# Delta layer of an eight-layer model: a head's preparation inside the preceding head's levels, and the recurrence's step ahead of the triangles' products

## Chip, cores and metric

One core of a Trainium2 chip runs the whole program in one launch. The metric is the device time of that launch in microseconds (us), the median of several runs.

## What is computed

Eight layers over 512 tokens of width 1024 in fp32; the seventh is the delta layer of this case. For each of 6 heads (width 128) and both directions of time it solves a gated delta rule. The reference, cut to that:

```python
g = jnp.cumsum(g, axis=-1)
decay = jnp.exp(jnp.where(tril, g[..., :, None] - g[..., None, :], NEG_INF))
k_beta = k * beta[..., None]
lmat = jnp.where(strict, jnp.einsum('bhnik,bhnjk->bhnij', k_beta, k) * decay, 0.0)
a = lmat + jnp.eye(DN_CHUNK)
sol = lax.linalg.triangular_solve(a, rhs, left_side=True, lower=True, unit_diagonal=True)
intra = jnp.where(tril, jnp.einsum('bhnik,bhnjk->bhnij', q, k) * decay, 0.0)
def step(state, inp):
    v_new = uc - jnp.einsum('bhck,bhkv->bhcv', wc, state)
    out = einsum(qc * exp(gc), state) + einsum(ac, v_new)
    state = state * exp(g_last) + einsum(kc * exp(g_last - gc), v_new)
o = o_fwd + o_bwd
o = o * lax.rsqrt(jnp.mean(o * o, axis=-1, keepdims=True) + EPS) * out_norm * jax.nn.silu(z)
```

## The kernel before

The kernel works with chunks of 128 tokens, 4 for each head (`TT = 4`, `P = 128`, `S = 512`, `NH = 6`), and with one list of instructions written out by hand for each engine (`pe`, `act`, `dve`, `pool` of `dn_layer`, L2231 to L2722). Semaphores tie them; each engine takes its own list strictly in order. PSUM has eight banks, `PS[:, 0..7, :]`.

The loop over h runs from 0 to 6. Turn h holds three things.

**Preparation of head h.** TensorE multiplies the gate column with a triangle to spread the cumulated gates (L2398, banks 2 and 3, one for each direction), forms keys by keys and keys by queries (L2405, banks 0 and 1), and turns values and keys (L2415, bank 7, one after the other). VectorE subtracts the columns and adds the causal mask (L2654), ScalarE takes the exponentials (L2499, L2501), VectorE weighs them with beta (L2660, L2664), multiplies with the key product to give NT (L2669) and with the query product to give AT (L2672). TensorE turns NT (L2424), ScalarE copies it to M (L2522). VectorE's two copies with a mask (L2677, L2679) put the neighbours of the diagonal into the unit triangles TT and Tm, which GpSimd has set to the identity (L2571, L2577). GpSimd also multiplies the queries with the gates (L2583, L2587).

**Levels 1 to 6 of head h** double the size of the inverted blocks. A level is four hops on TensorE for two halves g of the chunks: hops 0 and 1 multiply NT with Tm and M with TT into banks 0 and 1 (L2314, L2317); ScalarE copies a bank to XZ (L2528); hops 2 and 3 multiply XZ with Tm and TT into banks 2 and 3 (L2324, L2327); VectorE copies the result under a mask into Tm and TT (L2695, L2696), which the next level's hops read. Level 6 makes only TT. In level 1 a run of the mask is 2 elements, then 4, 8 and so on.

**Recurrence of head h-1**: four steps c, each for two directions, each in three hops (`recur_pe`): state products (L2346, L2348), the product of TT with the residual (L2355), the update and the output products (L2360, L2361). Between them stand VectorE's residual (L2686), ScalarE's scaling with beta (L2515) and VectorE's state (L2704, L2707), the last behind both halves' level copies. Step 0 stands in the preparation of head h, steps 1 to 3 in levels 1 to 3, a recurrence hop behind each of the level's hops 1, 2 and 3. After step 3 ScalarE squares the output in bank 6 (L2537), TensorE sums it with a matrix of ones over 128x512 (L2440), ScalarE takes the root (L2540), and VectorE at level 5 takes the reciprocal over 128x512 (L2713) and gates and splits the output (L2714 to L2718), ahead of its copies of level 6.

Turn 6 has only the recurrence of head 5. Behind it the output projection starts.

Of the kernel before, what the change touches and what calls it, by code (L numbers as in the profile page):

```python
# [14 lines left out]
F32 = mybir.dt.float32  # L15
# [3 lines left out]
ALU = mybir.AluOpType  # L19
# [3 lines left out]
P = 128  # L23
# [21 lines left out]
NH = 6  # L45
# [15 lines left out]
def program(nc, io, out):  # L61
    ctx = ExitStack()
    with ctx:
# [2167 lines left out]
        def dn_layer(l):  # L2231
            q = sig("dn", "conv gdve gact gcol mask gr prep eg D Dx nt at "
                    "vte qg ti head root ve rm")
# [22 lines left out]
                     W=([P, S],), S=([P, 2, P],), r=([P, 2, P],), vn=([P, 2, P],), sq=([P, S],)))  # L2256
            NT, M = hT_a[:, 5, :], hT_b[:, 5, :]
            Tm, XZ = hT_a[:, 6:8, :], hT_b[:, 6:8, :]
# [44 lines left out]
            def invert_pe(h, lv, hop):  # L2303
                t_ = nc.tensor
                g = hop % 2
                TTh = d_.TT[:, h % 2]
                if hop < 2:
# [3 lines left out]
                    if lv == 1 and g == 1:  # L2311
                        t_.wait_ge(q.at, 2 * h + 2)
# [17 lines left out]

            def recur_pe(h, c, hop):
                t_ = nc.tensor
                for d in range(2):
# [3 lines left out]
                    if hop == 0:  # L2337
                        if c == 0 and d == 0:
                            if h:
                                t_.wait_ge(q.os, B.os + h)  # L2340
                            t_.matmul(PS[:, 6, :], r.zr[0:1, :], r.zr[0:1, 0:1].to_broadcast([1, S]), start=True, stop=False)
# [7 lines left out]
                    elif hop == 1:  # L2349
                        if c:  # L2350
                            t_.wait_ge(q.rr, B.rr + j + 1)
                        elif d == 0:
                            t_.wait_ge(q.pc, joined(h, NL - 1, 1))
                        rhs = d_.r[:, d, :] if c else d_.v[:, h % 2, cc]
# [10 lines left out]
            def pe():  # L2365
# [23 lines left out]
                nh.pe()  # L2389
                for h in range(NH + 1):  # L2390
                    if h < NH:
                        t_.wait_ge(q.gdve, 4)
                        t_.wait_ge(q.nrm, L0 + 2 * h + 2)
                        for d in range(2):
                            if h:
                                t_.wait_ge(q.pc, joined(h - 1, NL - 1, d))
                            for c in range(TT):
                                mm = t_.matmul(PS[:, 2 + d, cs(c)], r.g[:, c, NH * d + h:NH * d + h + 1].to_broadcast([P, P]),  # L2398
                                               r.tri[:, d, :], start=True, stop=True)
                            mm.then_inc(q.gr, 1)  # L2400
                        if h == 0:
                            t_.wait_ge(q.nrm, L0 + 2 * NH)
                        for n, rhs in enumerate((HP + h, h)):
                            for c in range(TT):
                                mm = t_.matmul(PS[:, n, cs(c)], r.qkvT[:, HP + h, cs(c)], r.qkvT[:, rhs, cs(c)], start=True, stop=True)  # L2405
                            mm.then_inc(q.prep, 1)
                        if h:
                            t_.wait_ge(q.kte, B.kte + h)
                        if h >= 2:
                            t_.wait_ge(q.root, 2 * h - 2)  # L2410
                        for n in (2 * HP + h, HP + h):
                            if n < 2 * HP:
                                t_.wait_ge(q.vte, h + 1)
                            for c in range(TT):
                                mm = t_.transpose(PS[:, 7, cs(c)], r.qkvT[:, n, cs(c)], ident[:])  # L2415
                            mm.then_inc(q.prep, 1)
                    if h:
                        recur_pe(h - 1, 0, 0)
                        recur_pe(h - 1, 0, 1)
                    if h < NH:  # L2420
                        t_.wait_ge(q.nt, h + 1)
                        t_.wait_ge(q.eg, 2 * h + 1)
                        for c in range(TT):
# [404 lines left out]
```

## Time and profile before

| | us |
|---|---|
| median of 3 runs | 2932.04 (2931.57 to 2935.28) |
| the profiled execution's own time | 2930.64 |
| its span, first to last instruction | 2928.5 |
| TensorE busy in the span | 2623.7 |
| weight loads / VectorE / ScalarE / GpSimd busy | 2125.6 / 1449.2 / 1068.6 / 268.6 |
| mean granted TensorE clock | 0.935 |

The heads' loop of the delta layer runs from 2165.5 us (first decay product) to 2503.1 us (first product of the output projection). A product of 128x128 by 128x128 in fp32 stands in the trace as two records of MATMUL and two of LDWEIGHTS; a transposition stands as one. "MATMUL x8" is four products. The granted clock is a share of TensorE's 2.4 GHz: 1.00 is that level, 0.50 is 1.2 GHz, a value between them is a mean over both.

### The profile page before, as it was taken

The numbers are of one execution on the slowest core, as the hardware profiler recorded it, in microseconds if no ns is written. First come the engines' busy times: TensorE is split into PE (matmuls) and PEld (weight loads), VectorE is DVE, ScalarE is ACT, GpSimd is POOL, SyncE is SP. The second block draws the span as 40 slices with busy tenths as digits, with TensorE's granted clock in tenths as the row PEclk, the third lists the DMA queues.
The fourth block names the chain that finished last, engine by engine and source line by source line (L and its number), as shares of the span: only waits on it lengthen the run. The fifth ranks groups of instructions, "written<-read, shape, count | busy, mean of one in ns | idle before, by whom it ended". The sixth has DMA issues, their size and how long they took to land.

```text
span 2928.5 us, 33226 instructions
## 1 busy us (share of the span) xinstructions
PE 2623.7 (90%) x13178; PEld 2125.6 (73%) x13178; DVE 1449.2 (49%) x2374; ACT 1068.6 (36%) x1873; POOL 268.6 (9%) x420
## 2 busy tenths in 40 slices
PE   6898999999789989999789999999778687899998
PEld 4677777788357777877468888888547676688887
DVE  5667565653484556532335333257445555443422
ACT  3445432422463455444424222242433333332221
POOL 5233021020000132000000000010000100000000
PEclk7999999999799999999789999999779788999999
DMA  5522273364012311330103333232200000233332
GB/s 207 180 71 88 80 253 128 102 218 141 30 37 73 130 37 58 107 91 30 44 29 108 101 94 95 87 116 83 68 1 1 1 1 1 65 94 101 94 94 79
DMA packets 146227, 250.16 MB, mean 85 GB/s; under 512 B 15455, under 2 KB 65914, under 8 KB 145049
## 3 DMA queue, kind: packets, MB, share of 16 engines
q1 hardware_dynamic: 129008, 198.08, 21.8%
q0 software_dynamic: 14816, 48.31, 5.0%
q8 instruction: 105, 1.72, 0.2%
q10 hardware_dynamic: 2249, 1.65, 0.2%
q14 instruction: 49, 0.40, 0.0%
HBM read 245.84 MB, written 5.30 MB: 86 GB/s over the span
## 4 chain that ended last, share of the span: by engine, by line
PE 75%; DVE 10%; ACT 8%; DMA 4%; issue 2%; POOL 0%; SPq 0%; DVEq 0%; ACTq 0%
PE PS L218 19%; PE PS L220 18%; PE PS L219 18%; PE PS L985 2%; ACT tmp L752 1%; PE PS L2314 1%; PE PS L2317 1%; DMA hT_b<-in_w_mod 1%; PE PS L2327 1%; PE PS L2324 1%; PE PS L1760 1%; ACT w_hi L203 1%; PE PS L1445 1%; DVE x L808 1%; PE PS L1744 1%
## 5 line engine op out<-in xcount | busy, mean ns | idle before, releaser
L210 DVE TENSOR_TENSOR w_lo<-w_raw,w_hi 128x1024 fp32r<-128x1024 f32 (+1 forms) x344 | 412.5, 1206 | 779.1 <-ACT w_hi L203 777.9
L203 ACT ACTIVATE w_hi<-w_raw 128x1024 fp32r<-128x1024 f32 (+1 forms) x344 | 356.6, 1045 | 1039.3 <-DMA w_raw<-in_ffn_w_gate_up 308.0
L218 PE MATMUL PS<-hT_hi,w_hi 128*128 128x512 f32 (+1 forms) x1728 | 661.0, 383 | 21.5 <-DVE hT_lo L820 13.7
L220 PE MATMUL PS<-hT_hi,w_lo 128*128 128x512 f32 (+1 forms) x1728 | 652.7, 378 | 0.0
L219 PE MATMUL PS<-hT_lo,w_hi 128*128 128x512 f32 (+1 forms) x1728 | 652.3, 378 | 0.0
L218 PEld LDWEIGHTS PS<-hT_hi,w_hi 128*128 128x128 f32 x1728 | 331.0, 192 | 85.1 <-issue 19.3
L220 PEld LDWEIGHTS PS<-hT_hi,w_lo 128*128 128x128 f32 x1728 | 330.4, 191 | 59.4
L219 PEld LDWEIGHTS PS<-hT_lo,w_hi 128*128 128x128 f32 x1728 | 331.0, 192 | 56.8 <-issue 0.2
L218 PE MATMUL PS<-w_hi,hT_hi 128*128 128x512 f32 (+1 forms) x704 | 289.9, 412 | 35.3 <-DVE hT_lo L2722 9.1
L219 PE MATMUL PS<-w_lo,hT_hi 128*128 128x512 f32 (+1 forms) x704 | 278.4, 395 | 0.0
L220 PE MATMUL PS<-w_hi,hT_lo 128*128 128x512 f32 (+1 forms) x704 | 278.0, 395 | 0.0
L218 PEld LDWEIGHTS PS<-w_hi,hT_hi 128*128 128x128 f32 x704 | 140.9, 200 | 71.4 <-issue 15.8
L219 PEld LDWEIGHTS PS<-w_lo,hT_hi 128*128 128x128 f32 x704 | 141.1, 200 | 26.9 <-issue 1.8
L220 PEld LDWEIGHTS PS<-w_hi,hT_lo 128*128 128x128 f32 x704 | 140.1, 199 | 27.9
L517 DVE SCALAR_TENSOR_TENSOR macc<-mraw,cond,macc 128x512 f32<-128x512 f32 x160 | 122.0, 762 | 37.5 <-DMA mraw<-in_w_mod 34.7
L218 PE MATMUL PS<-w_hi,ffn_hi 128*128 128x512 f32 x352 | 139.4, 396 | 0.0
L219 PE MATMUL PS<-w_lo,ffn_hi 128*128 128x512 f32 x352 | 139.2, 396 | 0.0
L220 PE MATMUL PS<-w_hi,ffn_lo 128*128 128x512 f32 x352 | 139.2, 395 | 0.0
L462 POOL DMA_DIRECT2D mraw<-in_w_mod x160 | 86.3, 540 | 420.3 <-DVE macc L517 417.5
L985 PE MATMUL PS<-gla_E 128*128 128x128 f32 x448 | 62.6, 284 | 21.1 <-DVE gla_E L1204 21.0
L985 PEld LDWEIGHTS PS<-gla_E 128*128 128x128 f32 x448 | 58.4, 196 | 31.6 <-issue 29.3
L220 PEld LDWEIGHTS PS<-w_hi,ffn_lo 128*128 128x128 f32 x352 | 66.2, 188 | 15.9
(546 smaller groups left out, 3546.9 us busy)
## 6 DMA issues: line engine op xcount, KB each, us to landing
w_raw<-in_ffn_w_gate_up SPq DMA_DIRECT2D x176, 256.0 KB, 3.1
mraw<-in_w_mod POOLq DMA_DIRECT2D x160, 256.0 KB, 4.0
w_raw<-in_gla_w_in SPq DMA_DIRECT2D x48, 512.0 KB, 4.7
w_raw<-in_ffn_w_down SPq DMA_DIRECT2D x44, 512.0 KB, 3.8
w_raw<-in_fox_w_in SPq DMA_DIRECT2D x32, 512.0 KB, 4.3
w_raw<-in_sgu_w_in SPq DMA_DIRECT2D x24, 512.0 KB, 4.7
w_raw<-in_dn_w_in SPq DMA_DIRECT2D x24, 512.0 KB, 3.6
w_raw<-in_gla_w_out SPq DMA_DIRECT2D x16, 512.0 KB, 4.5
```

Source lines behind the costliest of these rows:

```text
L203: nc.scalar.activation(w_hi[:, n % NS, :, 0:m], w_raw[:, n % NS, :, 0:m], ACT.Copy).then_inc(w_hidone, 1)
L210: nc.vector.tensor_tensor(w_lo[:, n % NS, :, 0:m], w_raw[:, n % NS, :, 0:m], w_hi[:, n % NS, :, 0:m].bitcast(F32), ALU.subtract).then_inc( ...
L218: nc.tensor.matmul(o, l_hi, r_hi, start=start, stop=False)
L219: nc.tensor.matmul(o, l_hi, r_lo, start=False, stop=False)
L220: return nc.tensor.matmul(o, l_lo, r_hi, start=False, stop=stop)
L462: eng.dma_start(mraw[:, n % MS, 0, :], w[:, i % KT, m * BW:(m + 1) * BW]).then_inc(p_landed[n % MS], 16)
L517: nc.vector.scalar_tensor_tensor(out=acc, in0=mraw[:, n % MS, 0, :], scalar=cond[:, i % KT:i % KT + 1], in1=acc, op0=ALU.mult, op1=ALU.add ...
L752: ins = a.activation(tmp[:, k * P:(k + 1) * P], PS[:, 2 * t + k // 4, (k % 4) * P:(k % 4 + 1) * P], ACT.Identity, scale=nxt.scale[:, k:k + 1],
L808: v.tensor_tensor(x[:, t, :], x[:, t, :], y, ALU.add).then_inc(x_done, 1)
L985: mm = pe_.matmul(PS[:, l % 2, ts], a, m, start=True, stop=True)
L1445: t_.matmul(PS[0:nr, bank, :], sums[:, nr - per * n:2 * nr - per * n], sq(n), start=n == 0, stop=n == n_tiles - 1).then_inc(lens.sum, 1)
L1744: t_.matmul(PS[:, w.u % 3, 0:w.n], w.q, w.k, start=True, stop=True).then_inc(su.sc, 1)
```

## The change

The preparation of head n = h + 1 is spread over the levels of head h, on all engines. Preparation of head 0 stands before the loop. In each turn of level and hop TensorE takes the recurrence's hop first and the triangles' product after it; the recurrence has one step in each of levels 1 to 4. For this:

- NT, M and Tm exist twice (`NTs`, `Ms`, `Tms`), by the parity of the head. The decays live in M's place or in a spare tile, the second exponential has a tile of its own (`eb`).
- Banks: both directions' gates, the key product, the turned NT and the spread root all use bank 7; the query product bank 4; the turned values and keys bank 5; sums of squares four columns of bank 6.
- The neighbour copy of 128x512 is now two copies of 128x256, every second element of a row into one matrix each.
- Sums and root: four products with one column (`sums_pe`), root and reciprocal over 128x4, then four products that spread the reciprocal over a bank (`spread_pe`), one turn later. The gate is two products in place in `szT` (`gate_dve`, parts 0 and 2) with the split as part 3.

The diff of the parts that order the work; the bodies of the decay, products, weighing and key steps are those of before with the new banks and tiles:

```diff
-            NT, M = hT_a[:, 5, :], hT_b[:, 5, :]
-            Tm, XZ = hT_a[:, 6:8, :], hT_b[:, 6:8, :]
+            NTs, Ms = (d_.W[:], hT_a[:, 5, :]), (hT_b[:, 4, :], hT_b[:, 5, :])
+            Tms, XZ = (hT_a[:, 6:8, :], hf), hT_b[:, 6:8, :]
+            decay = lambda n, d: hT_a[:, 4, :] if d else Ms[n % 2]
...
+            def decay_pe(n, d):
+                t_ = nc.tensor
+                if d:
+                    t_.wait_ge(q.eg, 2 * n + 1)
+                elif n >= 3:
+                    t_.wait_ge(q.free, 2 * n - 4)
+                for c in range(TT):
+                    mm = t_.matmul(PS[:, 7, cs(c)], r.g[:, c, NH * d + n:NH * d + n + 1].to_broadcast([P, P]),
+                                   r.tri[:, d, :], start=True, stop=True)
+                mm.then_inc(q.gr, 1)
...
+            def sums_pe(k):
+                t_ = nc.tensor
+                t_.wait_ge(q.root, 3 * k + 1)
+                t_.wait_ge(q.free, 2 * k + 1)
+                for c in range(TT):
+                    mm = t_.matmul(PS[:, 6, c:c + 1], d_.sq[:, cs(c)], ones[:, 0:1], start=True, stop=True)
+                mm.then_inc(q.head, 1)
+
+            def spread_pe(k):
+                t_ = nc.tensor
+                t_.wait_ge(q.root, 3 * k + 3)
+                if k < NH - 2:
+                    t_.wait_ge(q.te, B.te + k + 3)
+                for c in range(TT):
+                    mm = t_.matmul(PS[:, 7, cs(c)], d_.rt[:, c:c + 1].to_broadcast([P, P]), ident[:], start=True, stop=True)
+                mm.then_inc(q.head, 1)
...
                 for h in range(NH + 1):
...
+                    n = h + 1
                     for lv in range(1, NL):
                         for hop in range(4):
+                            if h and lv <= TT and hop:
+                                recur_pe(h - 1, lv - 1, hop - 1)
                             if h < NH:
-                                if lv == 1 and hop == 3:
-                                    t_.wait_ge(q.eg, 2 * h + 2)
                                 invert_pe(h, lv, hop)
-                            if h and lv < TT and hop:
-                                recur_pe(h - 1, lv, hop - 1)
...
+                            if h >= 2 and lv == 1 and hop == 1:
+                                spread_pe(h - 2)
+                            if h and lv == 6 and hop == 1:
+                                sums_pe(h - 1)
+                            if n < NH:
+                                if lv == 4 and hop == 2:
+                                    products_pe(n, 0)
+                                if lv == 5 and hop == 1:
+                                    products_pe(n, 1)
+                                    rows_pe(n, 0)
+                                if lv == 6 and hop == 1:
+                                    rows_pe(n, 1)
+                        if n < NH:
+                            if lv == 1 or lv == 2:
+                                decay_pe(n, lv - 1)
+                            if lv == 5:
+                                upright_pe(n)
+                    if h == NH:
+                        spread_pe(h - 1)
...
                     for lv in range(1, NL):
...
+                        if h and lv <= TT:
+                            recur_act(h - 1, lv - 1)
+                        if n < NH:
+                            if lv == 2 or lv == 3:
+                                decay_act(n, lv - 2)
+                            if lv == 5:
+                                values_act(n)
+                            if lv == 6:
+                                upright_act(n)
+                                keys_act(n)
+                        if h and lv == 6:
+                            a.wait_ge(q.head, 3 * h - 1)
+                            a.activation(d_.rt[:], PS[:, 6, 0:TT], ACT.Sqrt, scale=1.0 / P, bias=r.eps[:]).then_inc(q.root, 1)
...
+                def neighbours_dve(n, side):
+                    mask = lvl[:, 0, :].rearrange("p (b h) -> p b h", h=2).unsqueeze(1).to_broadcast([P, TT, P // 2, 2])
...
+                    for e in range(2):
+                        rows = into[:, e, :].rearrange("p (c b h) -> p c b h", c=TT, h=2)[:, :, :, e]
+                        ins = v.copy_predicated(rows, mask[:, :, :, e], off.rearrange("p (c b h) -> p c b h", c=TT, h=2)[:, :, :, e])
...
                 for h in range(NH + 1):
...
+                    n, k = h + 1, h - 1
+                    for lv in range(1, NL):
+                        if h and 2 <= lv <= TT:
+                            residual_dve(k, lv - 1)
+                        if h >= 2 and lv <= 2:
+                            gate_dve(k - 1, lv + 1)
+                        if n < NH:
+                            if lv == 2 or lv == 3:
+                                decay_dve(n, lv - 2)
+                            if lv == 4 or lv == 5:
+                                weigh_dve(n, lv - 4)
+                            if lv == 5:
+                                keys_dve(n)
+                            if lv == 6:
+                                neighbours_dve(n, 0)
+                        if h < NH:
+                            level_dve(h, lv)
+                        if h and lv < TT:
+                            state_dve(k, lv - 1)
+                        if h and lv == 5:
+                            gate_dve(k, 0)
+                        if n < NH:
+                            if lv == 5:
+                                queries_dve(n)
+                            if lv == 6:
+                                neighbours_dve(n, 1)
+                        if h and lv == 6:
+                            gate_dve(k, 1)
```

## Rows read from the trace of the kernel before

**Rows 1.** The page's head.

```profile
span 2928.5 us, 33226 instructions
```

**Rows 2.** Turns of the loop: length, busy by engine (instructions), clock, DMA.

```profile
core 0: us, PE busy (x) PEld busy (x) DVE busy (x) ACT busy (x) POOL busy (x), PEclk, DMA share, GB/s
2186.20:2227.40 41.20, 32.91 (x233) 30.57 (x233) 22.05 (x44) 12.52 (x28) 3.85 (x4) 0.91 0.00 1
2227.40:2281.50 54.10, 40.17 (x292) 37.87 (x292) 31.35 (x62) 18.24 (x38) 5.02 (x6) 0.87 0.00 1
2281.50:2335.90 54.40, 40.52 (x292) 38.22 (x292) 31.24 (x62) 18.35 (x38) 5.02 (x6) 0.82 0.00 1
...
2390.50:2445.10 54.60, 40.74 (x291) 38.43 (x291) 31.23 (x61) 18.32 (x38) 5.02 (x6) 0.84 0.00 1
2445.10:2480.50 35.40, 30.81 (x235) 29.30 (x235) 18.62 (x39) 13.21 (x29) 0.00 (x0) 0.93 0.00 1
2480.50:2503.10 22.60, 12.69 (x71) 10.21 (x71) 12.21 (x22) 5.17 (x11) 0.00 (x0) 0.81 0.00 1
```

**Rows 3.** Chain of waits, turn 2: start, length, what ran.

```profile
2309.48 3.25 DVE dn_sq L2713
...
2316.04 3.75 PE PS L2398 x16
```

**Rows 4.** Shorter stretches, columns as in rows 2.

```profile
2196.68:2200.55 3.87, 3.87 (x34) 3.77 (x33) 1.55 (x4) 1.20 (x2) 0.00 (x0) 1.00 0.00 0
2344.11:2349.92 5.81, 5.81 (x55) 5.81 (x53) 3.14 (x10) 1.82 (x4) 0.00 (x0) 1.00 0.01 3
...
2371.00:2374.50 3.50, 3.45 (x18) 3.48 (x19) 1.36 (x5) 0.00 (x0) 0.00 (x0) 0.56 0.00 0
...
2224.50:2227.40 2.90, 0.11 (x1) 0.00 (x0) 2.90 (x3) 0.00 (x0) 0.00 (x0) 0.97 0.00 0
...
2228.00:2230.50 2.50, 2.50 (x14) 2.50 (x13) 0.00 (x0) 0.60 (x1) 0.00 (x0) 0.51 0.03 7
```

**Rows 5.** Small operations elsewhere: shortest/median/longest in ns, first and last start.

```profile
L504 PE MATMUL PS<-ones,macc x32: 352/352/352, 38.2 to 44.8; 128*128 128x1 f32 x32
...
L1160 DVE RECIPROCAL stat<-stat x8: 159/164/177, 196.9 to 1161.6; 128x4 f32<-128x4 f32 x8
```

**Rows 6.** Masked copies and the weighing, columns as in rows 5.

```profile
L2696 DVE COPY_PREDICATED dn_TT<-lvl,PS x72: 429/435/773, 2191.8 to 2480.1; 128x256 f32<-128x256 int8 x72
...
L2677 DVE COPY_PREDICATED dn_TT<-lvl,hT_a x6: 2347/2366/2370, 2181.6 to 2440.5; 128x512 f32<-128x512 int8 x6
...
L2679 DVE COPY_PREDICATED hT_a<-lvl,hT_b x6: 2555/2560/2560, 2183.6 to 2442.5; 128x512 f32<-128x512 int8 x6
...
L2660 DVE TENSOR_SCALAR dn_W<-dn_AT,dn_nbeta x24: 278/284/1290, 2175.0 to 2435.2; 128x128 f32<-128x128 f32 x24
```

**Rows 7.** Groups by line, turn 2: busy us, mean ns, idle before and its releaser.

```profile
L2398 PE MATMUL PS<-dn_tri,dn_g 128*128 128x128 f32 x16 | 3.8, 429 | 4.6 <-DVE dn_TT L2696 4.6
...
L2415 PE MATMUL PS<-ident,dn_qkvT 128*128 128x128 f32 x8 | 1.3, 279 | 0.7 <-ACT dn_v L2492 0.7
...
L2664 DVE SCALAR_TENSOR_TENSOR dn_W<-dn_AT,dn_nbeta,dn_W 128x128 f32<-128x128 f32 x4 | 2.1, 594 | 0.0
...
L2672 DVE TENSOR_TENSOR dn_AT<-dn_AT,PS 128x512 f32<-128x512 f32 x2 | 1.3, 678 | 0.0
L2714 DVE SCALAR_TENSOR_TENSOR tmp<-PS,vrows,dn_sq 128x512 f32<-128x512 f32 x1 | 0.8, 751 | 0.0
...
L2669 DVE TENSOR_TENSOR hT_a<-dn_W,PS 128x512 f32<-128x512 f32 x1 | 0.7, 686 | 0.0
...
L2499 ACT ACT_TABLE_LOAD x1 | 1.3, 1283 | 0.0
...
L2507 ACT ACTIVATE dn_ks<-PS,dn_kd 128x128 f32<-128x128 f32 x4 | 1.2, 408 | 0.0
```

**Rows 8.** Chain of waits at the start of the loop, columns as in rows 3.

```profile
2165.58 3.71 PE PS L2398 x16
...
2186.21 1.22 PE PS L2314 x4
```

More of the change, by code:

```diff
@@ new lines, in recur_act @@
+                def recur_act(k, step):
+                    for d in range(2):
+                        c = step if d == 0 else TT - 1 - step
+                        a.wait_ge(q.vm, B.vm + (TT * k + step) * 2 + d + 1)
+                        a.activation(d_.vn[:, d, :], PS[:, 4 + d, P:2 * P], ACT.Identity,
+                                     scale=r.beta[:, c, NH * d + k:NH * d + k + 1]).then_inc(q.ve, 1)
+                for d in range(2):
+                    decay_act(0, d)
+                values_act(0)
@@ new lines, in dve, with decay_dve @@
+                v.wait_ge(q.nrm, L0 + 2 * NH)
+                def decay_dve(n, d):
+                    v.wait_ge(q.gr, 2 * n + d + 1)
+                    for c in range(TT):
+                        ins = v.scalar_tensor_tensor(out=decay(n, d)[:, cs(c)], in0=PS[:, 7, cs(c)],
+                                                     scalar=r.G[:, d, c, n:n + 1], in1=r.cm[:, d, :],
+                                                     op0=ALU.subtract, op1=ALU.add)
+                    ins.then_inc(q.D, 1)
@@ new lines, in weigh_dve @@
+                def weigh_dve(n, d):
+                    W = NTs[n % 2]
+                    v.wait_ge(q.Dx, 2 * n + d + 1)
+                    for c in range(TT):
+                        if d == 0:
+                            ins = v.tensor_scalar(W[:, cs(c)], decay(n, 0)[:, cs(c)], r.nbeta[:, c, n:n + 1], None, ALU.mult)
+                        else:
+                            ins = v.scalar_tensor_tensor(out=W[:, cs(c)], in0=decay(n, 1)[:, cs(c)],
+                                                         scalar=r.nbeta[:, c, NH + n:NH + n + 1], in1=W[:, cs(c)],
+                                                         op0=ALU.mult, op1=ALU.add)
+                    then_dve(ins)
@@ new lines, in dve @@
+                for d in range(2):
+                    decay_dve(0, d)
+                for d in range(2):
+                    weigh_dve(0, d)
+                keys_dve(0)
+                queries_dve(0)
+                for side in range(2):
+                    neighbours_dve(0, side)
+                for h in range(NH + 1):
+                    n, k = h + 1, h - 1
[26 more added lines that the diff above has]
+                            gate_dve(k, 1)
@@ L2720, in dve @@
+                for part in (2, 3):
+                    gate_dve(NH - 1, part)
                 for n in range(2):
```

325 lines of the change are left out of this document (143 added, 182 removed).

## The prediction

> **What bounds the kernel now.** I read the page first: one core, a span of 2928.5 us [rows 1]. The change touches one stage, the delta layer's loop over its six heads, so I cut that stage into its turns [rows 2]. Each turn begins where head h's first level product starts. A turn with both a head's levels and the preparation of the next takes 54.1 to 54.6 us, four times (three stand in the rows); the first takes 41.2 us (no recurrence beside it), the last head's 35.4 us (nothing to prepare), and the tail, recurrence of head 5 alone, 22.6 us. In a 54.4 us turn TensorE is busy 40.5 us at a granted clock of 0.82, VectorE 31.2, ScalarE 18.4, GpSimd 5.0: no engine is full. The chain of waits says why [rows 3]. From 2281.5 to 2309.5 it runs on TensorE. Then it passes to VectorE's reciprocal over 128x512 (3.25 us) and the gate behind it; TensorE, through with level 6, waits 4.6 us for the last copy into TT queued behind them [rows 7]. From 2316.04 to 2335.88, 19.8 us, it is the preparation in series: decay products, exponentials, weights, two neighbour copies.
>
> The second thing to see is what TensorE costs inside the levels [rows 4]. A level with a recurrence step, 26 products of 128x128, took 5.81 us with TensorE busy all of it at clock 1.00: 0.2235 us a product. A level alone, 16 products, took 3.87, 0.3 more than the products. So levels are bound by TensorE already, and whatever is put among them costs its own TensorE time.
>
> **The change, part by part.** For a middle head (h = 2 to 4) TensorE now issues in one turn: 88 inversion products, 34 of the recurrence, 8 decay, 8 for the two key products, 4 for the spread row: 142 x 0.2235 = 31.7 us. Beside them 12 transposes, by the group of 8 at most 0.12 each at the full clock, 1.4; the zero product 0.25; and four one-column sums, 8 records. One column does not make a product cheap: 32 records took from 38.2 to 44.8 us at the low clock [rows 5], 0.21 each, so I estimate half at the full clock, 8 x 0.11 = 0.9. Together 34.3 us. That is the floor of a turn, by level: 6.95, 6.7, 5.8, 6.25, 5.4, 3.2.
>
> Removed from the path: the preparation as a stage (19.8 us), and the wide reciprocal. In its place stands one over 128x4, 0.164 us in the nearest row [rows 5], after a square root over 128x4.
>
> Now who comes late. I laid the four instruction queues side by side, with durations from [rows 6, 7] and 0.2 us for each handover.
> - Level 2: the recurrence's step now stands ahead of the second triangle product. Its state copy stands in VectorE's queue behind the copies of level 1: 0.4 us. The second decay product waits for ScalarE's exponential of the first (they share bank 7), behind the 1.28 us table load: 0.5.
> - Level 4: no decay product stands between level 3 and the step that needs the new state, which VectorE makes after both level copies: 0.7. Before the change two triangle products covered this. This is the cost of putting the recurrence first.
> - Levels 5 and 6: VectorE has in its queue the weights of the second direction (2.1 us), the key product (0.7), four level copies (0.44 each), the gate's first product (0.75), two query products (1.3), then neighbour copies, level 6, neighbour copies again. The last release the next turn. TensorE has 5.4 + 3.2 us of work there. VectorE reaches the gate 6.4 us after level 5 begins and the first neighbour copy 8.45 us after. TensorE loses 0.4 at level 5, 0.65 at level 6, and then waits for neighbours.
> - Next turn: the zero product waits for the square root, which stands on ScalarE behind eight scaled key copies (2.3 us) and a table load: 0.35.
>
> **The neighbour copies** are the one price I don't have. Before: 128x512 with the source in SBUF, 2.37 and 2.56 us, in runs of one element that alternate between two matrices [rows 6]. After: four copies of 128x256, stepping two elements, within one matrix. Bounds: 0.44 us, the median of a 256 copy with runs of four or more; 1.19, half of the old one. I take 0.75, what the 256 copies of level 1 (runs of two) show as the maximum in the same row. Then the neighbours of side one are done 12.35 us after level 5 began; TensorE had finished at 9.6: 2.95 us of idle time.
>
> The Trainium skill, "Vector Engine (DVE) Microarchitecture Reference", section "Measured stream behaviour on trn2", speaks against the cheap end: a port keeps its rate only for adjacent pairs of words, and small steps on sources or destination cost up to 2.5 ns a column. As an estimate from that page, 256 columns would take 0.6 to 0.7 us and the forecast fall by about 3 us. No row here has this shape.
>
> Stalls together: 0.4 + 0.5 + 0.7 + 0.4 + 0.65 + 2.95 + 0.35 = 5.95. A turn is 34.3 + 5.95 = 40.25.
>
> **The clock.** After an idle stretch of 2.9 us (2224.5 to 2227.4) the granted clock fell to 0.51 over 2228.0 to 2230.5; after the 4.6 us idle it was 0.56 over 2371.0 to 2374.5 [rows 4]. My idle of 2.95 is of that size. 3.5 us at about half rate lose 1.7 us. I include it: 42.0 us a turn.
>
> **GpSimd beside VectorE.** The weights' scaling took 0.284 us in the median and 1.290 at most [rows 6], one of each four caught while GpSimd multiplied the queries. GpSimd's multiplications move along, and in my layout meet the weights again, so I keep the 2.1 us for four [rows 7]. The Trainium skill, "SBUF — State Buffer", section "SBUF: two separate sides", has it as an exclusive lock of a shared port pair; the trace agrees in the one slow copy of four. Its reach to the neighbour copies, with two SBUF inputs, no row shows. By my layout GpSimd is idle there; a collision would cost up to 1.2 us a turn.
>
> **Other stretches.** Start: first decay product at 2165.5, first level product at 2186.2 [rows 8]. The copies shorten by 4.9 - 3.0 = 1.9, the exponentials no longer stand behind v's copy and a table load (1.9), the second half of the chain shortens by the products already waiting; against it decay 1 now waits for exponential 0. Queue by queue I get 2182.2: -4.0, bounds -1 and -6. First turn: levels 1 to 4 take 18.2 us of the present 24.8 (levels 5 and 6: 6.6), the fills add 1.6 beyond the slack, and levels 5 and 6 take 11.8 (12.55 without the gate's 0.75): 31.6 instead of 41.25: -9.65. Second turn: no spread product, no late gate: 40.8 for 54.0: -13.2. Third to fifth: 3 x 42.0 for 163.7: -37.7. Last head, nothing to prepare, level by level with the stalls and the clock: 8.1 + 6.2 + 5.8 + 6.0 + 4.1 + 3.3 = 33.5 for 35.4: -1.9. Tail: reciprocal 3.35 and first gate product off the path, but first gate product (0.95), sums (1.1) and spread (1.1) enter it: -1.8.
>
> **Sum.** 4.0 + 9.65 + 13.2 + 37.7 + 1.9 + 1.8 = 68.3. The stage moves next to nothing by DMA [rows 2], and the projection behind it starts when its last operand is split, so I shift it whole. The profiled execution's 2930.6 gives 2862.3. The median of the runs is 1.4 us higher: 2864.
>
> **Rivals.**
> 1. *TensorE's floor.* The queues fit, nothing waits, the clock holds: 34.3, 33.4 and 29.7 us for turns, 31.0 for head 5. That saves about 102 us: 2830. For it: the levels ran at full load before. Against: VectorE's 6.6 us at level 5 and the neighbours behind it. Chance 0.10.
> 2. *Cheap copies and a clock that holds*: 0.44 us copies shorten a turn by 1.2, the clock by 1.7: -16 us, 2848. Chance 0.20.
> 3. *The old rate stays*: 1.19 us a copy, six heads at 1.76: +10.6, 2874. Chance 0.15.
> 4. *It doesn't do what it says.* An engine's queue is in order; if a wait for a preparation step (bank 7 is used five times a turn, each use behind another engine's read) stands ahead of level work at every level, the preparation stays in series and only the gate's 4.6 us go: 5 x 5 = 25 us, 2907. Against it: GpSimd and ScalarE work less than half of a turn [rows 2]. Chance 0.08.
> 5. *Slower: the clock.* A turn holds 34.3 us of TensorE work at the full clock. If small stalls everywhere keep it at the low level (0.5), each microsecond of this work takes two. The turn had 14.4 us to give (54.4 - 40.0), so it turns slower once 42% of that work runs low; wholly low it would be 34.3 + 40.25 = 74.6, 5 x 20 = 100 us slower, 3030. Against: four levels in a row are full of work, and the levels of before, no fuller, ran at 1.00 [rows 4]. Chance 0.04.
>
> The forecast has 0.43: 2852 to 2874. The range of 2836 to 2888 leaves out the floor, most of rival 4 and rival 5. A measurement of this kernel can tell about 0.2% (6 us) from no change. Faster by more than that: 0.94; within it: 0.02; slower: 0.04.
>
> **What would show it.** Right: middle turns of about 42 us; a gap on TensorE before the first level product, released by VectorE's neighbour copies, of about 3 us; the clock near 0.5 for 3 us behind it; neighbour copies at 0.6 to 0.9 us; a 0.7 us wait before the recurrence's state product at level 4; no 3.3 us reciprocal. Wrong: a turn under 37 us (VectorE kept up), or above 46 (waits in bank 7 or on GpSimd, to be seen as decay or key products waiting on ScalarE).

## The result, and the profile after

The changed kernel takes 2857.48 us (2855.09 to 2861.78, 4 runs); the kernel before took 2932.12 us beside it. The ratio is 0.9745, interval 0.9728 to 0.9762. The profiled execution took 2855.09 us with a span of 2853.4 us, 75.1 less than before. The forecast was 2864, with a range of 2836 to 2888, and faster by over 0.2%. The kernel is faster by more than that, and its time lies in the range, 6.5 us under the forecast.

The turns of the loop in the changed kernel, cut as in [rows 2] (length, busy us and instructions of TensorE, its weight loads, VectorE, ScalarE and GpSimd, then clock, DMA share, GB/s):

```profile
2182.30:2212.40 30.10, 27.47 (x220) 26.78 (x220) 17.79 (x45) 11.91 (x26) 4.22 (x5) 0.94 0.00 1
2212.40:2252.60 40.20, 38.19 (x297) 36.64 (x297) 22.36 (x58) 15.34 (x36) 4.83 (x6) 0.92 0.01 1
2252.60:2292.90 40.30, 37.88 (x305) 36.44 (x305) 24.24 (x62) 17.86 (x39) 4.83 (x6) 0.96 0.01 1
2292.90:2331.70 38.80, 36.38 (x306) 34.93 (x306) 24.24 (x62) 17.88 (x39) 4.83 (x6) 1.00 0.00 1
2331.70:2373.40 41.70, 39.37 (x306) 37.71 (x306) 24.15 (x62) 17.89 (x39) 3.68 (x4) 0.92 0.01 2
2373.40:2406.50 33.10, 31.72 (x261) 30.13 (x261) 14.85 (x38) 10.90 (x24) 0.00 (x0) 1.00 0.00 1
2406.50:2428.10 21.60, 14.78 (x97) 12.45 (x95) 11.55 (x28) 4.64 (x11) 0.00 (x0) 0.85 0.00 1
```

A middle turn fell from 54.4 us to 38.8 to 41.7. TensorE is now busy nearly all of it. The three middle turns (the third, fourth and fifth of these rows) hold the same instructions and differ only in the clock: 1.00 in the shortest. Of the 15.6 us between 54.4 and 38.8, 11.5 are idle time of TensorE that is gone (13.9 before, 2.4 now). The other 4.1 are its own busy time, which fell from 40.5 to 36.4 although it issues 14 records more: the clock was 0.82 in that turn before [rows 2] and is 1.00 here.

From the first level product to the first product of the output projection the stage takes 245.8 us; before it took 316.9 (2186.2 to 2503.1). Below I compare kernels by this length first: the loop starts up to 8 us earlier or later from one execution to the next (2181.2 us in one execution of this kernel, 2182.3 in another, 2189.5 in a kernel with the same work ahead of it), which has nothing to do with the stage.

What TensorE waits for between 2182 and 2428 us (waiting line, releaser, us in total, times, longest):

```profile
PE PS L2313 <- DVE tmp L2734: 6.2, 3, 2.6
PE PS L2313 <- DVE hT_a L2734: 6.0, 3, 2.4
PE PS L2362 <- DVE dn_szT L2773: 1.6, 1, 1.6
PE PS L2396 <- DVE dn_S L2765: 1.3, 6, 0.2
PE PS L2337 <- ACT ajunk L2530: 1.1, 3, 0.4
```

L2313 is the first level product, L2734 the neighbour copies: six waits of 12.2 us. One of them, 2.4 us, ends where the stage begins; the five inside it take 2.64, 1.80, 1.80, 1.81 and 1.72 us. The rest is small. The wait for the last TT copy behind the reciprocal (4.6 in [rows 7]) is gone.

The end of a middle turn, from the timeline (start, length, what; in brackets the idle time before and its releaser):

```profile
2288.70 1.02 PE L2362 MATMUL PS<-ones,dn_sq 128*128 128x1 f32 x8
2288.74 1.16 POOL L2617 COPY hT_a<-ident 128x512 f32<-128x512 f32 x2 [2.52 <-PE PS L2313]
2289.66 1.41 DVE L2734 COPY_PREDICATED dn_TT<-lvl,hT_a 128x256 f32<-128x256 int8 x2
2290.05 1.06 PE L2326 MATMUL PS<-dn_TT,hT_b 128*128 128x128 f32 x8
2290.88 0.79 DVE L2746 COPY_PREDICATED dn_TT<-lvl,PS 128x256 f32<-128x256 int8 x2
2291.58 1.28 DVE L2734 COPY_PREDICATED tmp<-lvl,hT_b 128x256 f32<-128x256 int8 x2
2292.91 0.75 PE L2313 MATMUL PS<-tmp,hT_a 128*128 128x128 f32 x4 [1.80 <-DVE tmp L2734]
```

TensorE ends level 6 at 2291.1. VectorE still has the last level copies (L2746) and the second pair of neighbour copies in its queue, and the next head's first product waits 1.80 us.

### The profile page after: what moved, and what is told of

It reads as the page before. It is cut to its first block, busy times and chain, and to the rows that moved or that the text cites. A ratio compares the mean times of both kernels' runs of the same rounds, so it can differ in the third digit from the quotient of the medians.

```text
span 2853.4 us, 33398 instructions
## 1 busy us (share of the span) xinstructions
PE 2613.5 (92%) x13262; PEld 2121.6 (74%) x13262; DVE 1406.8 (49%) x2386; ACT 1063.3 (37%) x1871; POOL 269.0 (9%) x420
## 4 chain that ended last, share of the span: by engine, by line
PE 77%; DVE 8%; ACT 8%; DMA 4%; issue 2%; POOL 0%; SPq 0%; DVEq 0%; ACTq 0%
PE PS L218 20%; PE PS L219 19%; PE PS L220 19%; PE PS L985 2%; ACT tmp L752 1%; PE PS L2313 1%; DMA hT_b<-in_w_mod 1%; DVE x L808 1%; PE PS L1760 1%; PE PS L2326 1%; PE PS L2323 1%; PE PS L2316 1%; PE PS L1445 1%; ACT w_hi L203 1%; PE PS L1744 1%
## 5 line engine op out<-in xcount | busy, mean ns | idle before, releaser
L517 DVE SCALAR_TENSOR_TENSOR macc<-mraw,cond,macc 128x512 f32<-128x512 f32 x160 | 122.2, 764 | 39.0 <-DMA mraw<-in_w_mod 36.4
L2570 ACT ACTIVATE hT_b<-PS 128x512 f32<-128x512 f32 (+1 forms) x72 | 40.5, 562 | 113.5 <-PE PS L2316 99.0
```

Source lines behind the costliest of these rows:

```text
L517: nc.vector.scalar_tensor_tensor(out=acc, in0=mraw[:, n % MS, 0, :], scalar=cond[:, i % KT:i % KT + 1], in1=acc, op0=ALU.mult, op1=ALU.add ...
L2570: a.activation(XZ[:, g, 0:m], PS[:, g, 0:m], ACT.Copy).then_inc(q.xe, 1)
```

## The experiments

In the diffs minus is the changed kernel unless another is named. Where a kernel issues products or a reciprocal that nobody reads, its text says so; nothing else of the computation is left out anywhere.

**The same kernel again.**

> The changed kernel itself again, for the runs of the same chip. Both theories: 2855 to 2862 us. Theory A (the granted clock falls after TensorE's 1.8 us wait for the neighbour copies, in some turns and not in others) also expects turns between 38.8 and 41.7 us, with other turns the long ones than in the first profile. Rival B (the long turns are long because of their place) expects turns 1, 2 and 4 long again and 3 short.

2857.25 us (2854.61 to 2860.78), stage 245.8 us. Turns of 31.2, 38.7, 41.8, 38.8 and 40.2 us, where the first execution had 30.1, 40.2, 40.3, 38.8 and 41.7. Theory A is half right. The work is the same and the lengths differ, so the clock makes the difference; but it fell in the same turns again, the second, third and fifth, as rival B had it, and the fourth and the last head's stayed at 1.00. (38.7 is long for the second turn: it takes 37.3 without a fall, see the next run.) What changed is how long a fall lasts: about 7, 3 and 7 us in the first execution, 3, 7 and 3 in this one.

Here are stretches of 2 us in four turns of the first execution, columns as above. The second and fourth lie in turns without a fall:

```profile
2254.60:2256.60 2.00, 2.00 (x11) 2.00 (x11) 0.00 (x0) 0.31 (x1) 0.00 (x0) 0.50 0.00 0
2294.90:2296.90 2.00, 2.00 (x19) 2.00 (x19) 0.24 (x1) 0.61 (x2) 0.00 (x0) 1.00 0.00 0
2333.70:2335.70 2.00, 2.00 (x10) 2.00 (x11) 0.00 (x0) 0.02 (x1) 0.00 (x0) 0.50 0.04 8
2375.40:2377.40 2.00, 2.00 (x19) 2.00 (x19) 0.23 (x1) 0.60 (x2) 0.00 (x0) 1.00 0.00 0
```

All four begin some 2 us after the 1.7 to 1.8 us wait at a turn's start. TensorE is busy in all of them and issues 19 records of products in two stretches and 10 or 11 in the other two. So the same wait lets the clock fall from 1.00 to 0.50 in some turns and not in others. Why in these turns stays open: in the kernel with the order put back, below, it fell in the second, fourth and fifth turn, with the same waits of 1.7 to 2.6 us.

**The gap filled.**

```diff
+                            if lv == 6:
+                                for c in (0, 1, 2, 3, 0, 1, 2, 3):
+                                    t_.matmul(PS[:, 0, 256 + P * (c % 2):384 + P * (c % 2)], NTs[h % 2][:, cs(c)], ident[:], start=True, stop=True)
```

> Adds eight products without use (1.8 us at the full clock) behind the last triangle product of level 6, where TensorE waits 1.8 us for the neighbour copies. Theory A (that wait makes the granted clock fall in three of five turns, 1.5 to 2.9 us each): all turns at about 38.8 us, 4 to 8 us faster than the changed kernel although it does more work. Rival B (the clock falls for another reason, or not from this wait): no gain, or up to 2 us slower.

2851.41 us (2846.35 to 2856.89), ratio to the kernel before 0.9729 (0.9708 to 0.9749), stage 237.8 us, 8.0 less. Its turns 2 to 4:

```profile
2216.50:2253.80 37.30, 36.98 (x314) 35.73 (x314) 22.40 (x58) 15.32 (x36) 4.84 (x6) 1.00 0.01 1
2253.80:2292.50 38.70, 38.08 (x321) 36.64 (x321) 24.28 (x62) 17.79 (x39) 4.85 (x6) 1.00 0.00 1
2292.50:2331.30 38.80, 38.12 (x321) 36.68 (x321) 24.29 (x62) 17.88 (x39) 4.85 (x6) 1.00 0.01 1
```

Eight products without use most likely make the kernel faster. The turn does not get shorter than a clean one (VectorE is as late as before); only the falls are gone. Turn by turn that gives 0, 3.0, 1.5, 0, 3.0, and 0.5 in the last head and tail, together 8.0 us. The intervals of the two ratios overlap, so the gain in the whole time is likely, not certain; the absence of the falls is plain in the trace, which is one execution.

**The order put back**: triangles' product first, the recurrence's hop behind it.

```diff
-                            if h and lv <= TT and hop:
-                                recur_pe(h - 1, lv - 1, hop - 1)
                             if h < NH:
                                 invert_pe(h, lv, hop)
+                            if h and lv <= TT and hop:
+                                recur_pe(h - 1, lv - 1, hop - 1)
```

> Undoes the second half of the change: in each level and hop TensorE takes the triangles' product first, the recurrence's hop after it. Theory A (the recurrence is off the path either way; TensorE's work is the same): within 3 us of the changed kernel, the 0.2 us wait for the state at level 4 gone, nothing else. Rival B (the order is what lets the preparation fit in): the recurrence's values come 0.9 us later in each step, ScalarE and VectorE stand idle for them, and the turns grow by 1 to 3 us each: 5 to 15 us slower than the changed kernel.

2855.95 us (2848.55 to 2861.19), ratio 0.9737 (0.9714 to 0.9759), stage 243.3 us: no difference that can be told. The waits show why:

```profile
PE PS L2313 <- DVE tmp L2734: 6.2, 3, 2.6
PE PS L2313 <- DVE hT_a L2734: 6.0, 3, 2.4
PE PS L2337 <- ACT ajunk L2530: 3.8, 3, 1.3
```

The wait for the new state (L2396) is gone, as expected, but the second decay product, behind the level, now waits 1.28 us instead of 0.38 for ScalarE's exponential of the first. In a middle turn they cancel (38.9 us clean, against 38.8): level 3 begins 0.8 us later in the turn, and levels 4 and 5 together take 0.7 less. In the last head's turn, which has no decay products, putting the order back gains: the spread product of head 4 starts 31.8 us after the head's first product instead of 34.0, at clock 1.00 in both.

**The neighbour copies ahead**: of VectorE's level 6 copies and of the second query product. The core of it; a wait of the recurrence's first step is raised to cover the later query product.

```diff
                             if lv == 6:
                                 neighbours_dve(n, 0)
+                                neighbours_dve(n, 1)
...
                             if lv == 5:
-                                queries_dve(n)
+                                queries_dve(n, (0,))
                             if lv == 6:
-                                neighbours_dve(n, 1)
+                                queries_dve(n, (1,))
```

> VectorE makes the neighbour copies ahead of the copies of level 6 and of the second query product. Theory A (these copies are the last release of a turn): the wait ahead of the first level product shrinks from 1.8 to about 0.6 us, 6 us over five turns, and with it the clock's falls, up to 7 more: 6 to 13 us faster than the changed kernel. Rival B (something else is due at the same time, such as ScalarE's keys and root): under 2 us.

2855.7 us (2851.03 to 2857.03), ratio 0.974 (0.9721 to 0.9758), stage 245.3: the wait fell from 1.80 to 1.50 us only.

```profile
PE PS L2313 <- DVE dn_TT L2746: 7.9, 6, 2.1
```

The releaser has changed from the neighbour copies to the last copy into TT. Both count on the same semaphore `pc`, so a wait for the neighbours' count holds for every copy queued on it, whatever the order. That is a flaw of this experiment, and that it gained so little says nothing against the queue as the cause. So the next kernel gives the neighbour copies a semaphore of their own.

**The same with its own semaphore**, against the last kernel:

```diff
+                    if lv > 1:
+                        t_.wait_ge(q.pc, joined(h, lv - 1, g))
+                    elif g == 0:
+                        t_.wait_ge(q.nb, h + 1)
...
-                        ins.then_inc(q.pc, 1)
+                        ins.then_inc(q.nb, 1)
```

> The order of copies_first (both neighbour copies ahead of the copies of level 6 and of the second query product), but with a semaphore of their own, so that the first level product is not held by the count of the level copies. Theory A (the last release of a turn is the second neighbour copy, when nothing stands ahead of it): the wait shrinks from 1.8 to about 0.6 us, the clean turn from 38.8 to 37.6, and the clock falls in fewer turns or none: 6 to 12 us faster than the changed kernel, 2845 to 2851. Rival B (ScalarE's copy of the turned matrix, or its root, is due at the same time): the wait stays above 1.4 us and the time within 3 us of the changed kernel.

2851.42 us (2849.09 to 2857.35), ratio 0.9731 (0.9717 to 0.9746), stage 240.6. The interval overlaps the changed kernel's. The wait did not shrink to the expected 0.6 us, nor the turn to 37.6.

```profile
PE PS L2394 <- ACT dn_rt L2586: 3.7, 4, 1.3
PE PS L2316 <- DVE tmp L2737: 2.8, 3, 1.5
PE PS L2316 <- DVE hT_a L2737: 1.8, 2, 0.9
```

The wait for neighbours halved to 0.9 us in a middle turn, and the turn kept its length, 38.7 us at clock 1.00. The stage is shorter because the first turn's wait shrank (2.64 to 1.48) and because the clock fell in two turns, the second and the fifth, and not in three. The 0.9 us come back as a wait of the zero product (L2394) for ScalarE's root, which stands behind the scaled key copies and a table load. The predicted "root" term had been hidden behind the neighbours until then.

**The root ahead of the scaled keys**, against the last kernel:

```diff
                             if lv == 6:
                                 upright_act(n)
-                                keys_act(n)
                         if h and lv == 6:
                             a.wait_ge(q.head, 3 * h - 1)
                             a.activation(d_.rt[:], PS[:, 6, 0:TT], ACT.Sqrt, scale=1.0 / P, bias=r.eps[:]).then_inc(q.root, 1)
+                        if n < NH and lv == 6:
+                            keys_act(n)
```

> copies_own with ScalarE taking the square root ahead of the eight scaled key copies. In the trace of copies_own TensorE waits 0.9 us for that root before the zero product, a wait that stood behind the neighbour copies before. Theory A (the root was the next to be late): that wait goes, the clean turn falls from 38.7 to about 37.8: 3 to 5 us faster than copies_own, about 2847. Rival B (the keys, now 1.5 us later, or the copy of the first level product behind them, take its place): no gain.

2845.25 us (2844.12 to 2847.79), ratio 0.9708 (0.9694 to 0.9721), stage 233.6. The root wait is gone, and a middle turn takes 37.8 us at clock 1.00. Of the turns behind the first the clock fell in the second only, after a wait of 1.48 us.

```profile
2249.47:2287.28 37.81, 36.32 (x305) 34.87 (x306) 24.43 (x63) 17.62 (x39) 5.17 (x6) 1.00 0.00 1
2287.28:2325.11 37.83, 36.33 (x305) 34.90 (x306) 24.41 (x63) 17.63 (x39) 5.15 (x6) 1.00 0.00 1
```

**The second decay product moved into level 3**, behind its first hop, where the exponential is done; against the last kernel:

```diff
+                                if lv == 3 and hop == 0:
+                                    decay_pe(n, 1)
...
-                            if lv == 1 or lv == 2:
-                                decay_pe(n, lv - 1)
+                            if lv == 1:
+                                decay_pe(n, 0)
```

> root_first with the second decay product moved from the end of level 2 to level 3, behind its first triangle product. Theory A (TensorE waits 0.4 us a turn, 3.3 us once, for ScalarE's first exponential behind the table load): those waits go, 2 to 4 us faster than root_first. Rival B (the exponential is late by as much where it stands now, and VectorE's level 3 waits for the decay product): no gain.

2844.03 us (2840.91 to 2848.29), ratio 0.9707 (0.9693 to 0.9722), stage 233.0: the same as the last within the spread of the runs. The expected 2 to 4 us did not come. The wait did go and the turns at clock 1.00 shortened by 0.6 us each. The 3.3 us that the expectation counted in is the wait for the exponential in the preparation of head 0, ahead of the loop; the edit does not touch it, and it is 3.29 us in this trace too.

```profile
2180.18:2210.36 30.18, 28.71 (x220) 27.90 (x220) 16.72 (x43) 11.73 (x26) 4.32 (x5) 0.90 0.00 1
2210.36:2246.66 36.30, 35.18 (x298) 33.94 (x298) 22.62 (x59) 14.93 (x33) 5.16 (x6) 1.00 0.01 1
2246.66:2283.82 37.16, 36.04 (x306) 34.80 (x306) 24.41 (x63) 17.62 (x39) 5.16 (x6) 1.00 0.01 1
...
2390.90:2413.20 22.30, 15.49 (x95) 13.16 (x93) 11.46 (x28) 4.64 (x11) 0.00 (x0) 0.80 0.00 1
```

But the first turn took 30.2 us at a clock of 0.90 (29.0 at 0.94 in the last kernel) and the tail 22.3 at 0.80 (20.7 at 0.89). The low stretches, the first 6 us of the loop and the last 9 of the tail, lie ahead of and behind what the edit moves. In this execution most of what the turns gained went into the clock there. Whether the edit has a part in that is not shown: the first turn's fall is of either length, 3 or 7 us, in the two executions of the changed kernel as well.

**The same with four unused products** behind level 6, as in the filled gap:

> root_decay with four products without use (0.9 us) behind the last triangle product of level 6. Theory A (even the 0.9 us wait that is left lets the granted clock fall in some turns): all clean turns, 2 to 5 us faster than root_decay. Rival B (the clock holds over so short a wait): no gain, or 1 us slower.

2842.27 us (2835.28 to 2842.73), ratio 0.9691 (0.9675 to 0.9707), stage 233.4. Behind the first turn's start there is no fall up to the tail, but the last kernel's profile had none there either. Whether the filling adds anything here is unclear. This kernel and the last are 13 to 15 us faster than the changed kernel: the best found.

**The wide neighbour copy**, as before the change:

```diff
-                    for e in range(2):
-                        rows = into[:, e, :].rearrange("p (c b h) -> p c b h", c=TT, h=2)[:, :, :, e]
-                        ins = v.copy_predicated(rows, mask[:, :, :, e], off.rearrange("p (c b h) -> p c b h", c=TT, h=2)[:, :, :, e])
+                    wide = lvl[:, 0, :].rearrange("p (b h s) -> p b h s", h=2, s=1).unsqueeze(1).to_broadcast([P, TT, P // 2, 2, 1])
+                    ins = v.copy_predicated(mixed(into, 0, 0, TT), wide, off.rearrange("p (c b h s) -> p c b h s", c=TT, h=2, s=1))
```

> The neighbours in the form of the kernel before: one copy of 128x512 for each side, in runs of one element that alternate between the two matrices, in place of two of 128x256. Theory A (the copies are on the path at the end of each turn): 2.37 + 2.56 for 1.41 + 1.28, so 2.2 us more for each of five turns and 1.5 at the start: 13 us, and a wait of 4.0 us after which the clock falls in every turn, 3 to 8 more: 2870 to 2879. Rival B (the copies run beside other waits): under 4 us slower.

2877.72 us (2874.48 to 2879.04), ratio 0.9813 (0.98 to 0.9827), stage 263.7: 20 us slower, as expected. The neighbour wait and two middle turns:

```profile
PE PS L2313 <- DVE tmp L2733: 12.3, 3, 4.5
PE PS L2313 <- DVE hT_a L2733: 11.8, 3, 3.9
...
2258.40:2303.06 44.66, 40.11 (x306) 38.38 (x306) 26.21 (x60) 17.93 (x38) 4.83 (x6) 0.88 0.00 1
2303.06:2347.60 44.54, 40.00 (x306) 38.26 (x306) 26.19 (x60) 17.93 (x38) 4.83 (x6) 0.91 0.00 1
```

The wait grows by 2.1 us a turn (the two wide copies take 2.49 and 2.33 us in the median, for 1.41 + 1.28), and with 3.8 to 4.5 us of it the clock falls in every turn. The narrow form of the copy is worth these 20 us in the new order.

**A wide reciprocal** whose result nobody reads, ahead of the narrow one:

```diff
                         v.wait_ge(q.root, 3 * k + 2)
+                        then_dve(v.reciprocal(d_.sq[:], d_.sq[:]))
                         v.reciprocal(d_.rt[:], d_.rt[:]).then_inc(q.root, 1)
```

> VectorE takes a reciprocal over 128x512 ahead of the one over 128x4 (its result is not used), at the end of level 6. Theory A (the wide reciprocal costs what it delays, and here only the spread products wait for it): they start 3.3 us later, of which TensorE has 1.4 us of other work: 1.9 us a turn in turns 2 to 5 and 3.4 in the tail, 11 us slower than the changed kernel. Rival B (in the new order it is hidden): only the tail's 3.4. In the kernel before, the same instruction had TensorE waiting 4.6 us a turn.

2871.05 us (2865.7 to 2874.68), ratio 0.9791 (0.9774 to 0.9808), stage 260.3. The price is on the path: 13.6 us in the median.

```profile
PE PS L2371 <- DVE dn_rt L2778: 10.0, 5, 3.6
```

TensorE's spread product waits 0.6 us in the third turn, where the clock had fallen, and 1.9 us in the fourth, the fifth and the last head's, since other products stand ahead of it. In the tail it stands twice and waits 3.6 and 3.95 us, the last just behind the window of this line: there the 3.35 us reciprocal has no cover. In the turns with 1.7 to 1.8 us of wait for the neighbours and, 3 us later, 1.9 for the spread product the clock stayed at 1.00.

**The narrow root alone, in the kernel before**: sums with one column, root and reciprocal over 128x4, spread product and gate in place, everything else in the old order. The core of it, minus being the kernel before:

```diff
-                            t_.matmul(PS[:, 7, :], ones[:], d_.sq[:], start=True, stop=True).then_inc(q.head, 1)
+                            for c in range(TT):
+                                mm = t_.matmul(PS[:, 7, c:c + 1], d_.sq[:, cs(c)], ones[:, 0:1], start=True, stop=True)
+                            mm.then_inc(q.head, 1)
...
-                            then_dve(v.reciprocal(d_.sq[:], d_.sq[:]))
...
+                            v.wait_ge(q.spr, h)
+                            then_dve(v.tensor_tensor(hf[:, 0, :], hf[:, 0, :], PS[:, 7, :], ALU.mult))
```

> The kernel before with one part of the change alone: sums by four one-column products, root and reciprocal over 128x4, four spread products at level 5 and the gate as two products. Preparation stays a stage of its own. Theory A (of the 75 us most come from hiding the preparation): VectorE's gate shrinks from 5.9 to 2.6 us, TensorE's wait from 4.6 to about 1.3 and the spread costs 0.9: 2.4 us in each of five turns, and 2 in the tail: 12 to 17 us faster than before, 2915 to 2920. Rival B (the gate's wait and the clock behind it are the larger part): over 30 us faster than before.

2908.9 us (2907.89 to 2911.87), ratio 0.9922 (0.991 to 0.9935): 23 us, more than the 12 to 17 of the one theory and less than the over 30 of the other.

```profile
2276.20:2327.20 51.00, 39.78 (x306) 38.13 (x306) 28.49 (x62) 17.86 (x38) 5.02 (x6) 0.87 0.00 1
2327.20:2378.20 51.00, 39.85 (x305) 38.20 (x305) 28.38 (x61) 17.93 (x38) 5.02 (x6) 0.87 0.00 1
...
PE PS L2398 <- DVE dn_TT L2706: 6.7, 4, 1.7
```

Turns of 51.0 us for 54.4; TensorE waits 1.7 us for the last TT copy instead of 4.6. Of the 75 us, about 23 are what the root and gate alone give in the old order. The other 52 come with the preparation moved into the levels, the new place of the recurrence and the narrow neighbour copies together. No run has the narrow copies in the old order. There TensorE waited 2.84 us a turn for the second of the wide ones (2.85 in this kernel), so they would give a part of the 52 by themselves. The split holds for this order of adding the parts.

## Why the prediction came out as it did

**Which case.** The forecast's own mechanism: the preparation runs beside the levels, and the neighbour copies end last. Rival 1 (nothing waits, turns of 34.3 us) did not come; nor did rivals 4 and 5. In time the result lies between the forecast and rival 2 (2848), but for neither of rival 2's reasons: the copies were not cheap, and the clock did fall.

**Turn by turn**, gain predicted against measured: start 4.0 and 3.9; first turn 9.65 and 11.1; second 13.2 and 13.8; third to fifth 37.7 and 43.0; last head and tail 3.7 and 3.2. Sum 68.3 and 75.0. The start's agreement is partly luck: from the first decay product to the first level product it took 20.7 us before and 17.8 now, 2.9 less, and the other 1.1 us is that this execution came to the stage earlier. Most of the miss, 5.3 us, is in the third to fifth turn, and I take a clean one (2292.9 to 2331.7) apart by the starts of TensorE's groups.

**The floor, 34.3 us: right.** Inside the levels a product takes 0.22 to 0.225 us, a transpose 0.11, a one-column record 0.11 (eight from 2327.46 to 2328.34). One thing was missing: in level 1 the first products take 0.295 instead of 0.2235, and the zero product 0.41 instead of 0.25, 0.8 us together, at clock 1.00.

**The stalls, 5.95 us: too large.** What is left of the 38.8 is 4.5 us: level-2 state 0 (0.4 predicted), exponential 0.65 with the time until the products ahead of it are through (0.5), level-4 state 0.5 (0.7), level 5 0.25 (0.4), level 6 0.4 (0.65), neighbours 2.0 (2.95), root hidden (0.35), and level 1's 0.8. Over three turns the stalls make 4.4 us of the 5.3, and the clock, 4.4 for the predicted 5.1, most of the rest. The term that was mis-sized most is the neighbours'. It is a difference of two queues: I had VectorE done 12.35 us after level 5 began and TensorE 9.6; in the turn that starts at 2292.9 it was 11.1 and 9.15. VectorE's chain shows where its 1.2 us went (start, length on the chain; this is the end of the turn before, which is alike):

```profile
2288.55 1.19 DVE dn_AT L2721 x2
2289.74 1.33 DVE dn_TT L2734 x2
2291.07 0.60 DVE dn_TT L2746 x2
2291.67 1.20 DVE tmp L2734 x2
2292.91 0.75 PE PS L2313 x4
```

Two query products of 0.68 us each occupy 1.19 us, not 1.36; the first pair of neighbour copies has a record of 1.41 us, and the next instruction starts 1.22 after it (2289.66, 2290.88). In this chain the records of instructions that follow one another on VectorE overlap by 0.08 to 0.2 us. I added whole durations. For the 13 instructions behind VectorE's last wait for TensorE, from the level copies of level 5 on, they make 7.7 us; in the trace these take 6.6 (2325.01 to 2331.62). That is 1.1 us of the 1.2, in a difference of 2.75.

**The neighbour copies' price, 0.75 us: right.** All twenty-four, grouped by tile (shortest/median/longest in ns):

```profile
L2734 DVE COPY_PREDICATED dn_TT<-lvl,dn_W x6: 733/806/1067, 2178.9 to 2329.1; 128x256 f32<-128x256 int8 x6
L2734 DVE COPY_PREDICATED hT_a<-lvl,hT_b x6: 710/758/1064, 2180.3 to 2330.9; 128x256 f32<-128x256 int8 x6
L2734 DVE COPY_PREDICATED dn_TT<-lvl,hT_a x6: 732/810/1054, 2208.8 to 2370.7; 128x256 f32<-128x256 int8 x6
L2734 DVE COPY_PREDICATED tmp<-lvl,hT_b x6: 714/744/772, 2211.1 to 2372.5; 128x256 f32<-128x256 int8 x6
```

The estimate from the Trainium skill, "Vector Engine (DVE) Microarchitecture Reference", section "Measured stream behaviour on trn2", was 0.6 to 0.7; the traces give 0.71 at the least and 0.74 to 0.81 in the median, so the page was near and a little low.

**The clock, 1.7 us a turn: right in sum, not in kind.** The filled gap gives 8.0 us for five turns and tail; 5 x 1.7 is 8.5. But the fall did not come in every turn: it came in three of five, costing 1.5 to 3.0 us where it came. That the sum fits is luck. The term was drawn from idle stretches of 2.9 and 4.6 us; the waits were 1.7 to 2.6, and no row ahead of the prediction showed what the clock does behind those.

**GpSimd beside VectorE.** The collision at the neighbours that the prediction allowed for came where GpSimd's identity copies ran late, in the first turn:

```profile
2208.51 1.48 POOL L2617 COPY hT_a<-ident 128x512 f32<-128x512 f32 x2 [2.51 <-PE PS L2313]
2209.51 1.05 DVE L2734 COPY_PREDICATED dn_TT<-lvl,hT_a 128x256 f32<-128x256 int8 x1
```

A 0.73 us copy took 1.05, the one before it 0.95, and GpSimd's pair took 1.48 for 1.16. Ahead of the loop, where four copies of each engine run side by side, they follow one another every 0.87 us on both from the second on, where a VectorE copy alone takes 0.51 from start to start and GpSimd's 0.55. So each engine is held back, but for less than the other's length. The Trainium skill ("SBUF — State Buffer", section "SBUF: two separate sides") has an exclusive lock for the whole instruction. Taken with these starts it would give 1.06 us; whether the lock covers only a part of each, or the two share, no run here shows. The 1.2 us a turn that I had given as the upper bound were too much: the pair of copies lost 0.5 us.

**The recurrence's step first.** The 0.7 us at level 4 that I put down as its cost was 0.2 of wait, 0.5 with the time until the products ahead of it are through, and putting the order back moved the loss to the exponential instead. What this part of the change did for the time by itself is within the noise of these runs.

## What to carry to other kernels

Once work is moved into another engine's shadow, the turn is set by the difference of two queues, so small errors per instruction matter: add starts to starts, not durations, and list every operation that stands ahead of the one releaser. Before reordering, look which semaphore carries the count that is waited for; when it is shared, the order among the copies that count on it decides nothing. When one wait is removed, name the next that ends last: here neighbours, then the root, then the exponential, and the three edits on them, measured one on top of the other, brought 6, 6 and 1 us in the medians (the first and the last within overlapping intervals) and 5.2, 7.0 and 0.6 us of the stage.

## What the runs showed of the hardware

- The same wait of 1.8 us on a TensorE that was busy otherwise was followed by a fall of its clock from 2.4 to 1.2 GHz in some turns and not in others. Two executions of one program had the falls in the same turns, with other lengths (3 to 7 us). The length of the wait alone does not decide: behind 1.7 to 1.8 and then 1.9 us the clock held in three turns of the kernel with the wide reciprocal; with 0.9 us for the neighbours and 0.8 for the root 1.2 us later it fell in one of three middle turns, and with 0.9 alone in none. With waits of 3.8 to 4.5 us it fell in every turn. Eight products nobody reads, placed in the gap, kept it at 2.4 GHz in all five.
- A product with one column costs 0.11 us a record at 2.4 GHz, as one with 128 columns does.
- A masked copy on VectorE and a plain copy on GpSimd, at the same time in SBUF, slow each other down by 0.2 to 0.35 us each.
